# The opening of a one-core decoder kernel: blank TensorE products, one norm vector turned first, chunk 0 in two halves, and a later row of square sums

## What is computed

```python
def rmsnorm(x, gain):
    xf = x.astype(jnp.float32)
    y = xf * lax.rsqrt(jnp.mean(xf * xf, axis=-1, keepdims=True) + NORM_EPS)
    return (y * gain.astype(jnp.float32)).astype(x.dtype)

hn = rmsnorm(h, attn_norm[0])                 # h = x, 256 x 1024
proj = hn @ hgrn_w_in[0]                      # 1024 x 4096
q, f_raw, i_in, o_gate = jnp.split(proj, 4, axis=-1)
f = lbf + (1.0 - lbf) * jax.nn.sigmoid(f_raw) # lbf from softmax and cumsum over hgrn_lb
```

## Time and profile before

| | us |
|---|---|
| median of three runs | 1359.82 |
| lowest and highest run | 1353.86, 1361.48 |
| span of the profiled execution | 1352.8 |
| TensorE busy in it | 1307.0 |
| first instruction of TensorE | 8.01 |
| first product of chunk 0 | 14.69 |
| first product of chunk 1 | 23.28 |
| first product of the experts' loop | 472.79 |

### The profile page before, as it was taken

One profiled execution on the slowest core, in us unless ns is written; L12 is line 12 of the kernel. 1 busy time (PEld: TensorE's weight loads), 2 busy tenths in 40 slices (PEclk: granted clock), 3 DMA queues, 4 the chain that ended last, 5 costly groups with the idle time before them and its releaser, 6 DMA issues.

```text
span 1352.8 us, 32458 instructions
## 1 busy us (share of the span) xinstructions
PE 1307.0 (97%) x14601; PEld 826.4 (61%) x14601; DVE 362.6 (27%) x537; ACT 243.2 (18%) x364; POOL 53.5 (4%) x47
## 2 busy tenths in 40 slices
PE   6998999999999699999999999999999999999998
PEld 6997899988777433644654653563473464465244
DVE  5875555554776501101101101100100110110111
ACT  5463544433733100000000000000000000000000
POOL 0001000000000031000000000000000000001600
PEclk9998999999999799999999999999999999999999
DMA  9972465555521698799999999999999999999996
GB/s 323 350 261 64 143 193 185 186 198 191 212 95 63 279 362 335 302 419 370 417 420 409 415 420 413 410 420 419 405 419 420 403 419 420 407 417 419 417 416 250
DMA packets 114310, 442.51 MB, mean 327 GB/s; under 512 B 9396, under 2 KB 55812, under 8 KB 83460
## 3 DMA queue, kind: packets, MB, share of 16 engines
q1 hardware_dynamic: 108016, 424.75, 80.1%
q10 hardware_dynamic: 4820, 11.53, 2.3%
q0 software_dynamic: 1344, 4.20, 0.8%
HBM read 434.12 MB, written 12.08 MB: 330 GB/s over the span
## 4 chain that ended last, share of the span: by engine, by line
PE 90%; DVE 4%; DMA 3%; ACT 2%; issue 1%; ACTq 0%; SPq 0%; POOL 0%; DVEq 0%
PE bank L1705 40%; PE bank L1717 21%; PE bank L1348 8%; PE bank L1349 8%; PE bank L1350 8%; DMA raw<-in_moe_w_up 2%; DMA dn<-in_moe_w_down 1%; PE bank L1605 1%; PE bank L1553 1%; PE bank L1486 1%; DVE w_lo L838 0%; ACT w_hi L571 0%; DMA vecs<-in_hgrn_lb 0%; ACT ht_hi L598 0%; PE bank L1673 0%
## 5 line engine op out<-in xcount | busy, mean ns | idle before, releaser
L1705 PE MATMUL bank<-raw,xT 128*32 128x512 f32 (+1 forms) x4608 | 440.2, 539 | 2.8 <-DMA raw<-in_moe_w_up 2.1
L1705 PEld LDWEIGHTS bank<-raw,xT 128*32 128x32 f32 x4608 | 174.8, 110 | 260.2 <-issue 251.8
L1717 PE MATMUL bank<-dn,hidT 128*32 128x256 f32 x5376 | 291.9, 379 | 0.7 <-DMA dn<-in_moe_w_down 0.7
L1717 PEld LDWEIGHTS bank<-dn,hidT 128*32 128x32 f32 x5376 | 203.1, 110 | 89.8 <-issue 2.4
L1317 DVE TENSOR_TENSOR e_hid<-e_silu,bank 128x512 f32<-128x512 f32 (+1 forms) x48 | 26.9, 617 | 541.2 <-PE bank L1705 541.2
L838 DVE TENSOR_TENSOR w_lo<-raw,w_hi 128x2048 fp32r<-128x2048 f32 x62 | 141.7, 2290 | 111.3 <-ACT w_hi L571 111.3
L1705 PE MATMUL bank<-up_more,xT 128*32 128x384 f32 (+1 forms) x1536 | 150.9, 539 | 0.0
L1348 PE MATMUL bank<-ht_hi,w_hi 128*128 128x256 f32 x480 | 136.2, 284 | 4.2 <-DVE w_lo L911 2.7
L1349 PE MATMUL bank<-ht_lo,w_hi 128*128 128x256 f32 x480 | 135.5, 282 | 0.0
L1350 PE MATMUL bank<-ht_hi,w_lo 128*128 128x256 f32 x480 | 135.4, 282 | 0.0
L571 ACT ACTIVATE w_hi<-raw 128x2048 fp32r<-128x2048 f32 x62 | 118.5, 1915 | 50.3 <-PE bank L1350 50.3
(11 more groups left out here) (262 smaller groups left out, 830.8 us busy)
## 6 DMA issues: line engine op xcount, KB each, us to landing
dn<-in_moe_w_down SPq DMA_DIRECT2D x112, 1024.0 KB, 12.6
raw<-in_moe_w_gate SPq DMA_DIRECT2D x48, 1024.0 KB
raw<-in_moe_w_up SPq DMA_DIRECT2D x48, 1024.0 KB
raw<-in_moe_w_gate SPq DMA_DIRECT2D x48, 768.0 KB
raw<-in_moe_w_up SPq DMA_DIRECT2D x48, 768.0 KB
up_more<-in_moe_w_gate SPq DMA_DIRECT2D x16, 1024.0 KB
up_more<-in_moe_w_up SPq DMA_DIRECT2D x16, 1024.0 KB
raw<-in_hgrn_w_in SPq DMA_DIRECT2D x15, 1024.0 KB, 13.1
```

The costliest lines, as they stand in the source:

```text
L1705: ins = nc.tensor.matmul(out_banks[j][GTOK * c:GTOK * c + GTOK, 0:w], xT[:, j, kt, :], chunk[:, c], start=kt == 0, stop=kt == KT - 1)
L1717: ins = nc.tensor.matmul(banks[6 + j // 2][GTOK * c:GTOK * c + GTOK, 256 * (j % 2):256 * (j % 2) + 256], hidT[sup][:, g, m, :], dn[:, i % ...
```

## The change

Five edits, all in the opening:

1. VectorE's first instruction sets one 128 x 128 block of `eT` to zero, and TensorE begins with ten products of this block with itself into a bank that is later overwritten (float32, 128 columns each).
2. `attn_norm` is loaded by itself, first on ScalarE's queue, into rows of `bias_row`; TensorE turns these 16 rows by themselves ahead of `x`, and the other 48 rows behind `x`. VectorE copies the 48 columns behind the split of chunk 1.
3. Chunk 0 runs in two halves of the contraction: both column halves over blocks 0 to 3, and then both over blocks 4 to 7. The number of products is the same.
4. On ScalarE the rounding of chunk 1 moves ahead of the square sum of the second tile and of the exponential for the lower bound; on VectorE the split of chunk 1 moves ahead of the lower bound's arithmetic.
5. `spread_row(0)` moves from behind chunk 0 to behind chunk 1.

```diff
+            act.dma_start(bias_row[:, 0:P], a["attn_norm"].rearrange("l (r c) -> (l r) c", c=P)).then_inc(gain_loaded, 16)
             act.dma_start(const[:, 0:P], a["shape_constants"][:, 0:P]).then_inc(ident_loaded, 16)
-            for dst, src in ((vecs[0:16, :], a["attn_norm"].rearrange("l (r c) -> (l r) c", c=P)),
-                             (vecs[16:32, :], a["ffn_norm"].rearrange("l (r c) -> (l r) c", c=P)),
-                             (vecs[32:40, :], a["kv_norm"].rearrange("(r c) -> r c", c=P)),
-                             (vecs[40:64, :], a["hgrn_lb"].rearrange("l (r c) -> (l r) c", c=P))):
+            for dst, src in ((vecs[0:16, :], a["ffn_norm"].rearrange("l (r c) -> (l r) c", c=P)),
+                             (vecs[16:24, :], a["kv_norm"].rearrange("(r c) -> r c", c=P)),
+                             (vecs[24:48, :], a["hgrn_lb"].rearrange("l (r c) -> (l r) c", c=P))):
...
             nxt[0] = 1
+            round_to(LEAD - 1)
             act.wait_ge(x_loaded[1], 16)
             norm_stats(0, [1])
             act.wait_ge(lb_logit, 1)
             nc.scalar.activation(lb[:, 0:3, :], lb[:, 0:3, :], ACT.Exp).then_inc(lb_exp, 1)
-            round_to(LEAD - 1)
...
+            nc.vector.memset(eT[:, 0, 0:P], 0.0).then_inc(blank_ready, 1)
             nc.vector.memset(eps[:, :], EPS).then_inc(eps_ready, 1)
-            turn_copy(cols[:, :], 64)
+            turn_copy(cols[:, 0:16], 16)
...
             nxt[0] = 1
+            rest_to(LEAD - 1)
+            turn_copy(cols[:, 16:64], 48)
+            dve.wait_ge(turn_free, 2)
...
-            rest_to(LEAD - 1)
...
+            pe.wait_ge(blank_ready, 1)
+            for _ in range(10):
+                nc.tensor.matmul(banks[0][:, 0:P], eT[:, 0, 0:P], eT[:, 0, 0:P], start=True, stop=True)
             pe.wait_ge(ident_loaded, 16)
-            pe.wait_ge(vecs_loaded, 16 * 4)
-            nc.tensor.transpose(turn_bank()[:, 0:64], vecs[:, :], const[0:64, K_ID:K_ID + 64]).then_inc(turned, 1)
+            pe.wait_ge(gain_loaded, 16)
+            nc.tensor.transpose(turn_bank()[:, 0:16], bias_row[:, 0:P], const[0:16, K_ID:K_ID + 16]).then_inc(turned, 1)
...
+            pe.wait_ge(vecs_loaded, 16 * 3)
+            nc.tensor.transpose(turn_bank()[:, 0:48], vecs[:, :], const[0:48, K_ID:K_ID + 48]).then_inc(turned, 1)
+
+            def first_features(bank):
+
+                wh, wl = split_view(w_hi, 0, 256), split_view(w_lo, 0, 256)
+                for part in range(2):
+                    if part:
+                        pe.wait_ge(split_ready, 1)
+                    else:
+                        pe.wait_ge(first_lo, 1)
+                    for half in range(2):
+                        cut, dst = slice(P * half, P * half + P), bank[:, 256 * half:256 * half + 256]
+                        for k in range(4 * part, 4 * part + 4):
+                            if half == 0 and k % 2 == 0:
+                                pe.wait_ge(fresh_lo, k // 2 + 1)
+                            nc.tensor.matmul(dst, wh[:, k, cut], ht_hi[:, k, :], start=k == half == 0, stop=False, skip_group_check=True)
+                            nc.tensor.matmul(dst, wh[:, k, cut], ht_lo[:, k, :], start=False, stop=False, skip_group_check=True)
+                            ins = nc.tensor.matmul(dst, wl[:, k, cut], ht_hi[:, k, :], start=False, stop=k == KT - 1, skip_group_check=True)
+                ins.then_inc(chunk_used, 1)
...
             for c in range(14):
                 project(c)
-                if c == 0:
+                if c == 1:
                     spread_row(0)
-                if c == 1:
```

More of the change, by code:

```diff
@@ L141, in build_program @@
         const = sb(ctx, "const", [P, K_END])
-        vecs = sb(ctx, "vecs", [64, P])
+        vecs = sb(ctx, "vecs", [48, P])
         cols = sb(ctx, "cols", [P, 64])
@@ L299, in build_program @@
         vecs_loaded = sem("vecs_loaded")
+        gain_loaded = sem("gain_loaded")
+        blank_ready = sem("blank_ready")
         first_full = sem("first_full")
@@ L384, in build_program @@
         OUT_BANKS = [[banks[2], banks[3]], [banks[0], banks[4]]]
-        TURN_ATT = 2 + HEADS + 4 + TT + 4 + 4 * KVH
+        TURN_ATT = 3 + HEADS + 4 + TT + 4 + 4 * KVH
         GROUPS = ((0, 0), (0, 1), (1, 0), (1, 1))
@@ L644, in _ @@
             nc.scalar.activation(lb[:, 0:3, :], lb[:, 0:3, :], ACT.Exp).then_inc(lb_exp, 1)
-            round_to(LEAD - 1)
-            ta[0] += 2
+            ta[0] += 3
             flatT = lambda buf: buf[:, :, :].rearrange("p h t -> p (h t)")
@@ L1393, in to_features @@
             def to_features(c, bank, hi, lo, fresh=None):
-                if c > 0:
-                    pe.wait_ge(split_ready, c + 1)
+                pe.wait_ge(split_ready, c + 1)
                 wh, wl = split_view(w_hi, c, 256), split_view(w_lo, c, 256)
@@ L1401, in to_features @@
                             pe.wait_ge(fresh_lo, fresh[k])
[L1402 to L1406, removed]
                         cut = slice(P * half, P * half + P)
@@ L1462, in project @@
                 bank = proj_bank(c)
-                if c < 8:
-                    to_features(c, bank, ht_hi, ht_lo, {k: k // 2 + 1 for k in range(0, KT, 2)} if c == 0 else None)
+                if c == 0:
+                    first_features(bank)
+                elif c < 8:
+                    to_features(c, bank, ht_hi, ht_lo)
                 else:
```

## The result

The changed kernel takes 1401.74 us (median of four runs, 1400.73 to 1404.7), the kernel before 1359.82 us beside it (median of three runs): ratio 1.032, 95% interval 1.0295 to 1.0343. A fourth run of the kernel before took 2776.87 us in a slow state of the chip and is left out, as is one of 2298.34 us of a later kernel. The change makes the kernel 3% slower; I had forecast 1360.4 us and a range that ended at 1364. The profiled execution spans 1399.5 us against 1352.8, so 46.7 us have to be found.

What follows compares the result with a forecast made beforehand. TensorE was taken to bound the kernel, with VectorE's chain setting the projection's end: 1.4 later, less 0.34, less 0.5 slack, gives +0.6 us; 1359.8 + 0.6 = 1360.4 us, range 1354 to 1364.

Steps and rivals of the forecast that it cites:

- All behind the projection I take as moved by the same: After the projection: everything later, the experts' loop included, shifts by the projection's own 0.6 us; no further term.
- my cases: Whole kernel: low clock with absorbed lead 0.58, high clock 0.17, lead kept 0.12, late blanks 0.07, clock drop 0.06.
- Loads and turns: Opening: blanks take 4.4 us, TensorE turns from 5.5 instead of 8.0 us, first product at 12.2 instead of 14.69.
- The clock: Chunk 0's products: low level from 12.2 us for 4.4 us (3.0 to 5.4), costing 2.2 us (1.5 to 2.7).
- the likeliest case: Opening and projection: low clock and absorbed lead, 1359.7 to 1360.9 us, chance 0.58.
- The row and the absorbed lead: Projection: inverse roots copied 1.4 us later, at 25.8; TensorE's 3.4 us lead lost waiting for chunks 8 and 9; ends +0.6.
- TensorE's lead: Projection: 3.4 us ahead at line 1476, expected to be absorbed; rival that it is kept, 1356.4 us, chance 0.12.
- The clock drop: Projection: TensorE's new stalls before chunks 8 and 9 lower the clock, adding 3.4 us: 1363.8 us, chance 0.06.
- my reading in the prediction: Opening: turns in transpose mode don't count for the clock gate, so they would not hold up what the blanks raised.

Runs made afterwards that it cites:

- s = 34: Changed kernel with 8 blank products instead of ten, 34 TensorE instructions (s) more than before ahead of the loop: 1400.93 us, one run.
- the change with 214 fillers: Changed kernel plus 214 do-nothing TensorE instructions (fulfilled waits) ahead of the loop, 256 more than before in all: 1359.70 us, ratio 1.0014.
- before with 90, 128 and 170 fillers: Kernel before plus 90, 128 or 170 do-nothing TensorE instructions ahead of the loop: 1423.62, 1370.63 and 1361.66 us, one run each.
- before with 42: Kernel before plus 42 do-nothing TensorE instructions ahead of the loop, nothing of the change in it: 1402.56 us, ratio 1.034.
- s = 0, 2, 26, 30 and 256: TensorE instructions added ahead of the loop: kernel before; no blanks (1361.86 or, reordered, 1355.03 us); 6 blanks, reordered (1358.51); 7 blanks (1367.50); change plus 214 do-nothing instructions (1359.70).
- s = 42: 42 TensorE instructions more than before ahead of the loop: the changed kernel (1401.74 us), or kernel before plus 42 do-nothing ones (1402.56 us).
- with 7 and with 6 blanks: Changed kernel with 7 blanks: 1367.50 us; with 6 blanks, the row back behind chunk 0 and chunks 8 and 9 split earlier: 1358.51 us.
- Without blanks: Changed kernel without its ten blanks: 1361.86 us; also with the row back behind chunk 0 and chunks 8 and 9 split earlier: 1355.03 us.

## Why the prediction was wrong

**The step that failed** is one sentence: "All behind the projection I take as moved by the same". It was argued from data and semaphores (the wait of 0.9 us, the loads), and for those it held: the loop begins 2.6 us later and none of its loads came late. It had no place for the program itself as something that has to arrive. In its place the runs showed that the packet with the loop's head moved 2.6 to 2.8 us after each return instead of 3 us ahead of it, which made waits of 4.1 to 4.3 us at seven returns and, with the low clock behind them, 46 us. I counted ten blanks, their time and their clock, but not their instructions. The page of before had what was needed to ask: 119 instruction packets, and a loop of 1440 products a pass. None of my cases had a term for it, so the range excluded the outcome. It wasn't a rival that I priced wrongly; it was missing. Whether it would strike couldn't have been read from the trace of before alone without knowing where the packets' edges lie; with 42 more instructions a chance of some 4 in 10 would have been fair, an estimate from what the runs now show: by the straight line, waits of over 1.5 us stand from s = 34 to about 145 of the 256 places. The base was off as well, by less: in 17 to 23 runs beside the experiments the kernel before had medians of 1356.85 to 1358.39 us, and the forecast started from 1359.8.

**Loads and turns** held, a little late: the blanks took 4.64 us, from 1.03 to 5.67 (forecast 4.4), but the identity landed at 6.27, not by 5.3, so the first turn is at 6.31 instead of 5.5. TensorE then made up for it, with 16 turns in 1.97 us at the high level (3.67 before) and the first product at 11.74 (forecast 12.2).

**The clock** was the likeliest case in size, and the reading behind it was half right. Products of chunk 0 ran at the high level from 11.74 to 13.23, at the low one to 16.65, then high: 3.4 us low and 1.7 us lost, where I had 4.4 and 2.2. The windows of after over this stretch:

```profile
12.00:14.00 2.00, 2.00 (x16) 2.00 (x16) 2.00 (x5) 1.71 (x2) 0.00 (x0) 0.81 1.10 348
14.00:16.00 2.00, 2.00 (x12) 2.00 (x11) 1.31 (x2) 2.00 (x3) 0.00 (x0) 0.50 1.10 347
```

The first rise of the clock is at 6.41 us, just behind the blanks; the turns ran at the high level. The level fell again at 13.23, behind an idle stretch of 3.08 us and 1.5 us after the products had begun. The prediction had taken the low level as there from the first product on. In the change with 214 fillers it was so: the clock fell at 11.17.

**The row and the absorbed lead** held: copy at 25.00 (forecast 25.8), line 1499 at 24.90 (25.7), waits of 2.19 us before chunk 8 and 1.3 before chunk 9 (2.5 and up to 2). The scores came 0.4 us later than before, where I had +0.6, though both are less than the 1 us by which the unchanged opening varies. That the moved copy is what costs, is shown by undoing it (2.5 us) and by splitting chunks 8 and 9 earlier (another 1.3). TensorE's lead came through only with such an order.

**The clock drop**, my rival for slower, did occur: behind the stall before chunk 8 the clock fell at 61.02 for 3.4 us. The projection had room for it: TensorE still waited 1.3 us for the split of chunk 9 behind it. As a term of the total it is nothing beside the loop, and my time for it, 1363.8, was not what made the kernel slower.

**The rest to the loop**, +2.2 us, isn't shown to come from the change. After has a stretch of 3.4 us at the low level at 375.05, where before has none; the granted clock was 0.66 in a window of 5 us that has 1.00 before. That is 1.7 of the 2.2 us. But before with 90, 128 and 170 fillers has such a stretch too, at 372.61, 372.80 and 376.44, and before with 42 has none, though the opening and the work in between are the same. In these four kernels the loop begins at 475.58, 473.22, 476.81 and 472.88 us. What decides it, the runs don't tell; it stays open, and it is about as large as what the opening can win.

## What to carry to other kernels

In front of a long loop like this one (2895 TensorE instructions a pass), every instruction added or taken away can move its return over a packet's edge. Compare the wait on issue before the loop's first product, and the moment at which the packet of the instruction queue moves, before believing any time. To judge an edit elsewhere in such a kernel, hold the number of instructions ahead of the loop on that engine the same, or a multiple of 256 apart, with waits that are already fulfilled; without that, ten blank products looked like 3%. And where a lead is won on one engine, ask which engine's chain lets it through: here the copy of one row and the place of two splits were worth more than ten blank products.

## What the runs showed of the hardware

- A return over 2895 TensorE instructions waited from 0 to 5 us at its head by its place in a packet of 256: nothing at s = 0, 2, 26, 30 and 256, then 4.2 to 5.0 at 34, 4.1 to 4.3 at 42, 2.9 at 90, 2.0 at 128, 0.7 at 170. The branch itself took 5.0 us at s = 42 and 0.4 at s = 0 (first return).
- With such a wait, the head's first product came 2.8 to 2.9 us behind the beginning of its packet's move.
- The packet behind the head's let TensorE go on 4.9 to 6.0 us after the head's first product. If the head's packet held less work than that, there was a second wait: 3.5 to 4.9 us behind 8 products, 0.7 to 1.2 behind 38, 0.4 to 0.9 behind 40, and none behind 53 (s = 0 or 256). Behind 32 products (s = 42) it was 0.2 to 0.7 us at three of the seven returns, where the low clock had been short, and none at the others.
- A wait of 4 us at the head brought 3.4 or 6.8 us at the low clock. In the changed kernel the level fell from 1.8 us ahead of the head's first product to 0.4 us behind it. With 90, where two waits stand close together, the low stretch at the first two returns was 10.2 us.
- Leaving the loop cost something of its own with 7 and with 6 blanks. In both a packet moved right at the end (at 1352.85 and 1345.58), and TensorE went on 2.4 and 2.5 us behind that: with 7 a wait of 2.3 us on issue, with 6 one of 2.04 us where before has 1.16. The clock was low for 6.8 us from there.
- Turns alone raised the clock, against my reading in the prediction and against the rule of the Trainium skill that it cites ("TensorE: Matmul & The Clock Gate", Part 4). Without blanks the clock's first record, at 9.54 us, is a rise, and nothing but turns had run since 6.26; in before with 128 fillers it is at 10.99, and the 16 turns take 3.33 us where they took 3.67. Before with 90 and with 170 fillers show the same (10.79 and 11.21). In before, and with 42 fillers, they hadn't done so: there the first rise is at 20.28 and 20.51. It is of no use here: an idle stretch of 3 us follows, and the clock is low again soon after the products begin.
